# The next layer's first modulation, moved from GpSimd in attention to VectorE in the up projection

## The reference

```
c_act = silu(c)
for l in range(2):
    mod = c_act @ ada_w[l] + ada_b[l]          # ada_w[l] is 1024 x 6144
    sh1, sc1, g1, sh2, sc2, g2 = split(mod, 6)
    h = rmsnorm(x, norm1_g[l]) * (1 + sc1) + sh1
    proj = h @ w_in[l]                          # a scan, a latent attention, a window attention
    y = concat(y_ssd, y_mla, y_swa) @ w_out[l]
    x = x + g1 * y
    h = rmsnorm(x, norm2_g[l]) * (1 + sc2) + sh2
    u = causal_dwconv(h @ ffn_w_up[l])          # width 3, 2 x 2816 channels
    a, b = split(u, 2)
    x = x + g2 * ((silu(a) * b) @ ffn_w_down[l])
return rmsnorm(x, final_norm_g)
```

## Time and profile before

| | |
|---|---|
| three runs, median (lowest to highest) | 2300.6 us (2298.91 to 2301.53) |
| profiled execution | 2302.88 us |
| its span from the first to the last instruction | 2301.1 us |
| mean granted TensorE clock, share of full | 0.988 |
| busy: TensorE, VectorE, ScalarE, GpSimd | 98%, 70%, 48%, 45% |
| DMA traffic | 317.13 MB, mean 138 GB/s |

### The profile page before, as it was taken

One profiled execution on the slowest core, in us unless ns is written; L12 is line 12 of the kernel. 1 busy time (PEld: TensorE's weight loads), 2 busy tenths in 40 slices (PEclk: granted clock), 3 DMA queues, 4 the chain that ended last, 5 costly groups with the idle time before them and its releaser, 6 DMA issues.

```text
span 2301.1 us, 31154 instructions
## 1 busy us (share of the span) xinstructions
PE 2255.3 (98%) x11401; PEld 1852.8 (81%) x11401; DVE 1608.6 (70%) x2242; ACT 1103.9 (48%) x1817; POOL 1027.3 (45%) x664
## 2 busy tenths in 40 slices
PE   6999999999999999999999999999989999999998
PEld 5888878887788888888878787788878888888887
DVE  7885467449866676778898744762796666667886
ACT  5355557434444444444543564772444444444455
POOL 3222369445987777300002224153399777760000
PEclk7999999999999999999999999999999999999999
DMA  9742243342343333477457221224322333337763
GB/s 334 279 135 69 65 119 120 110 141 62 104 128 99 108 104 103 161 278 257 149 193 260 71 69 60 52 83 134 106 78 93 117 94 115 94 129 269 255 203 115
DMA packets 271302, 317.13 MB, mean 138 GB/s; under 512 B 33614, under 2 KB 188033, under 8 KB 270384
## 3 DMA queue, kind: packets, MB, share of 16 engines
q1 hardware_dynamic: 269359, 312.11, 41.8%
q10 hardware_dynamic: 1072, 2.23, 0.4%
q0 software_dynamic: 720, 0.81, 0.1%
HBM read 248.37 MB, written 62.54 MB: 135 GB/s over the span
## 4 chain that ended last, share of the span: by engine, by line
PE 88%; DVE 6%; issue 2%; DMA 1%; SPq 1%; POOL 1%; ACT 0%; DVEq 0%; POOLq 0%; ACTq 0%
PE bank L1579 31%; PE bank L1135 19%; PE bank L1594 17%; PE bank L1192 7%; PE bank L1470 2%; PE bank L1435 1%; PE bank L1351 1%; DVE hLo L2246 1%; PE bank L1398 1%; SPq L539 1%; PE bank L1399 1%; DVE xT L2240 1%; PE bank L1400 1%; PE bank L1391 1%; PE bank L1282 1%
## 5 line engine op out<-in xcount | busy, mean ns | idle before, releaser
L1055 POOL TENSOR_TENSOR wLo<-raw,wHi 128x1024 fp32r<-128x1024 f32 x66 | 164.1, 2487 | 407.3 <-ACT wHi L1057 407.3
L1780 POOL TENSOR_TENSOR prodLo<-comb,prodHi 128x512 fp32r<-128x512 f32 x160 | 234.3, 1471 | 123.8 <-ACT prodHi L1097 123.8
L1579 PE MATMUL bank<-tHi,prodHi 128*128 128x512 f32 x640 | 250.2, 391 | 4.8 <-DVE tLo L2659 4.1
L1579 PE MATMUL bank<-tLo,prodHi 128*128 128x512 f32 x640 | 249.6, 390 | 0.0
L1579 PE MATMUL bank<-tHi,prodLo 128*128 128x512 f32 x640 | 249.5, 390 | 0.0
L1594 PE MATMUL bank<-gateHi,downHi 128*128 128x512 f32 x616 | 240.3, 390 | 0.0
L1594 PE MATMUL bank<-gateHi,downLo 128*128 128x512 f32 x616 | 239.7, 389 | 0.0
L1594 PE MATMUL bank<-gateLo,downHi 128*128 128x512 f32 x616 | 239.7, 389 | 0.0
L1097 ACT ACTIVATE prodHi<-comb 128x512 fp32r<-128x512 f32 x160 | 100.5, 632 | 248.8 <-PE bank L1579 229.5
L2604 DVE SCALAR_TENSOR_TENSOR ub<-bank,ffp,ub 128x1023 f32<-128x1023 f32 x88 | 112.8, 1282 | 141.9 <-ACT ub L2053 140.3
L1579 PE MATMUL bank<-hHi,prodHi 128*128 128x512 f32 x480 | 187.1, 390 | 6.1 <-POOL prodLo L1780 3.5
(11 more groups left out here) (431 smaller groups left out, 5417.1 us busy)
## 6 DMA issues: line engine op xcount, KB each, us to landing
raw<-in_ffn_w_up_dram SPq DMA_DIRECT2D x88, 512.0 KB, 4.8
gateRaw<-gateOut SPq DMA_DIRECT2D x154, 256.0 KB, 4.3
adaE<-in_ada_w_dram SPq DMA_DIRECT2D x64, 512.0 KB, 6.1
gateOut<-gateSums SPq DMA_DIRECT2D x22, 1024.0 KB, 5.5
raw<-in_w_in_dram SPq DMA_DIRECT2D x34, 512.0 KB, 4.2
downRaw<-in_ffn_w_down_dram SPq DMA_DIRECT2D x66, 256.0 KB, 3.7
raw<-in_w_out_dram SPq DMA_DIRECT2D x28, 512.0 KB, 3.8
downCols<-in_ffn_w_down_dram SPq DMA_DIRECT2D x24, 512.0 KB, 3.6
```

The source lines that it names most:

```text
L1055: eng.tensor_tensor(lo[:], raw[slot][:], fview(hi[:]), ALU.subtract).then_inc(s["split_lo"], 1)
L1579: last = mm(o, w[idx][:, c0], moving(idx, kp, hi), start=kp == 0 and q_ == 0, stop=kp == 3 and q_ == 2)
L1780: pool.tensor_tensor(sLoW[idx][:], product_source(js, idx), fview(sHiW[idx][:]), ALU.subtract).then_inc(s["us_lo"], 1)
```

## The change

`load_ada`, `ada_products`, `ada_sum` and their place in attention are taken out. In layer 0's up projection, `load_next` loads 32 blocks of 128 x 512 in pairs behind the other transfers of SyncE's step, `next_product` makes two of them a step on VectorE (js 2 to 17) between result 6 and the taps, and after every eighth turns the sum in 32 x 32 blocks and reduces it to 16 columns. At the end of the stage four matmuls (`next_sums`) sum over the partitions and ScalarE copies 16 columns to `mod`. The new tiles lie in the upper halves of `hLo`, which are free by then, and beside the parameter rows. The stores of rstd for the scan, which stood among the loads of `load_ada`, now stand behind the second output pack in both layers.

```
-NEXT_AT = (23, 24) and load_ada, ada_sum, ada_products with their calls
+NEXT_TILES = 4 * KT
+NEXT_JS = 2
+    nextw = [place(f"nextAda{i}", [P, HALF], F32, R[8 + i] + 2 * K) for i in range(2)]
+    foldN = place("foldNext", [P, 2, 32], F32, at["x"] + 29 * K)
+    nexta = place("nextSum", [P, HALF], F32, R[10] + 2 * K)
+    nextt = place("nextTurned", [P, HALF], F32, R[11] + 2 * K)

+            def load_next(r):
+                c, k = divmod(r, KT)
+                if r < 2:
+                    sp.wait_ge(s["pack_used"], nth("pack_used", D0))
+                else:
+                    sp.wait_ge(s["ada_used"], nth("ada_used", r - 1))
+                sp.dma_start(nextw[r % 2][:], ada_next[:, k * P:(k + 1) * P, c * HALF:(c + 1) * HALF].rearrange("o p m -> (o p) m")).then_inc(s[f"ada_loaded{r % 2}"], 16)

                 load_up(j + 1)
                 if j % 2:
                     store_sums((j - 3) // 2)
+                if onward and 0 <= j - NEXT_JS - 2 < NEXT_TILES // 2:
+                    load_next(2 * (j - NEXT_JS - 2))
+                    load_next(2 * (j - NEXT_JS - 2) + 1)

+            def next_sums():
+                pe.wait_ge(s["ada_part"], nth("ada_part", 9))
+                for r in range(4):
+                    mm(bank[1][32 * r:32 * r + 32, 448:448 + 2 * KT], quad[:], foldN[:].rearrange("p j c -> p (j c)")[:, r:2 * 32:4], start=True, stop=True)

                         pe.wait_ge(s["up_tap"], nth("up_tap", 4 * (FT - 1)))
+                        next_sums()
                         transpose_params(pe, prow1)

                         act.wait_ge(s["params_transposed"], nth("params_transposed", 1))
+                        A(mod[:, 0:2 * KT], bank[1][:, 448:448 + 2 * KT], ACT.Copy).then_inc(s["mod_rest"], 1)

+            def next_product(r):
+                c, k = divmod(r, KT)
+                dve.wait_ge(s[f"ada_loaded{r % 2}"], nth(f"ada_loaded{r % 2}", 16 * (r // 2 + 1)))
+                if k == 0:
+                    dve.tensor_scalar(nexta[:], nextw[r % 2][:], cact[:, 0:1], None, ALU.mult).then_inc(s["ada_used"], 1)
+                else:
+                    dve.wait_ge(s["ada_used"], nth("ada_used", r))
+                    dve.scalar_tensor_tensor(out=nexta[:], in0=nextw[r % 2][:], scalar=cact[:, k:k + 1], in1=nexta[:],
+                                             op0=ALU.mult, op1=ALU.add).then_inc(s["ada_used"], 1)
+                if k == KT - 1:
+                    dve.wait_ge(s["ada_used"], nth("ada_used", r + 1))
+                    link(dve.transpose(nextt[:], nexta[:]))
+                    dve.tensor_reduce(foldN[:, c // 2, 16 * (c % 2):16 * (c % 2) + 16], nextt[:].rearrange("p (c i) -> p c i", i=32),
+                                      AX.X, ALU.add).then_inc(s["ada_part"], 1)

                 if js:
                     result(js - 1, 6)
+                if onward and 0 <= js - NEXT_JS < NEXT_TILES // 2:
+                    next_product(2 * (js - NEXT_JS))
+                    next_product(2 * (js - NEXT_JS) + 1)
                 taps(j - 1, 1)
                 taps(j - 1, 0)
                 result(js, 0)
...
                 if n == 10 and onward:
+                    dve.wait_ge(s["mod_rest"], nth("mod_rest", 2))
                     first_modulation(dve)
```

More of the change, by code:

```diff
@@ L787, in load_pack @@
                     sp.dma_start(raw[n % 2][:].rearrange("p (k m) -> p k m", k=KT), w[:, :, m * P:(m + 1) * P]).then_inc(sem, 16)
[L789 to L802, removed]
             def load_rope_tables():
@@ L896, in _ @@
                     load_rope_tables()
-                    if onward:
-                        load_ada(range(2))
                     place_query_rope()
-                if n == N_OUT0 and onward:
-                    load_ada(range(2, ADA_PACKS))
-                    sp.wait_ge(s["ada_used"], nth("ada_used", ADA_PACKS))
-                if n == N_OUT0 + 2 and not onward:
+                if n == N_OUT0 + 2:
                     store_rstd()
@@ L1193, in half_step @@
                 return last
-            def ada_sum(j, ms=range(KT)):
-                pe.wait_ge(s["ada_used"], nth("ada_used", KT * (j - 3)))
-                acc = (nt[0], nt[1])[j - 4]
-                to = half(2, 1)[:, 384:384 + KT]
-                for m in ms:
-                    last = mm(to[:, m:m + 1], acc[:, m * P:(m + 1) * P], caus01[:, P - 1:P], start=True, stop=True)
-                if ms[-1] == KT - 1:
-                    last.then_inc(s["ada_part"], 1)
+            def next_sums():
+                pe.wait_ge(s["ada_part"], nth("ada_part", 9))
+                for r in range(4):
+                    mm(bank[1][32 * r:32 * r + 32, 448:448 + 2 * KT], quad[:], foldN[:].rearrange("p j c -> p (j c)")[:, r:2 * 32:4], start=True, stop=True)
             def mod_sums(_):
@@ L1422, in transposes @@
                     pe.transpose(half(2, 1)[0:2 * NB, 384:512], rst[:], ident[:])
-                if u in NEXT_AT and onward:
-                    ada_sum(4 + NEXT_AT.index(u))
                 for part in range(2):
@@ L1671, in _ @@
         def _(pool):
-            def ada_products():
-                pool.wait_ge(s["mn_sum"], nth("mn_sum", 1))
-                pool.wait_ge(s["ada_part"], nth("ada_part", 5))
-                for r in range(ADA_PACKS):
-                    j, k = divmod(r, KT)
-                    acc, w = nt[j][:], raw[r % 2][:]
-                    pool.wait_ge(s[f"ada_loaded{r % 2}"], nth(f"ada_loaded{r % 2}", 16 * (r // 2 + 1)))
-                    ck = cact[:, k:k + 1].to_broadcast([P, D])
-                    if k == 0:
-                        pool.tensor_tensor(acc, w, ck, ALU.mult).then_inc(s["ada_used"], 1)
-                    else:
-                        pool.tensor_tensor(w, w, ck, ALU.mult).then_inc(s["ada_prod"], 1)
-                        pool.wait_ge(s["ada_prod"], nth("ada_prod", r - j))
-                        pool.wait_ge(s["ada_used"], nth("ada_used", r))
-                        pool.tensor_tensor(acc, acc, w, ALU.add).then_inc(s["ada_used"], 1)
             def scan_gate(ch):
@@ L2528, in beside_probs @@
                     dve.tensor_copy(rstd_row[:], sums[0:2 * NB, 384:512]).then_inc(s["sd_rstd"], 1)
-                if u in NEXT_AT and onward:
-                    n = NEXT_AT.index(u)
-                    dve.tensor_copy(mod[:, n * KT:(n + 1) * KT], sums[:, 384:384 + KT]).then_inc(s["mod_rest"], 1)
             least(0)
```

13 lines of the change are left out of this document (5 added, 8 removed), and 4 rows, old and new, of the table PER_LAYER.

## The result

The changed kernel takes 2330.14 us (median of 4 runs, 2326.83 to 2332.04), the kernel before 2301.07 us (4 runs, 2298.91 to 2304.38): a ratio of 1.0116, 95% interval [1.0104, 1.0127]. It is slower, and by more than the prediction's range allows (2295 to 2321 us). The execution that was traced (span 2325.1 us) is the fastest of the four, 2326.83 us, so the trace places 24 us of the 29 that the medians show. The three longer runs list a lower mean granted clock, 0.985 to 0.989 against 0.990; no trace places their further 3.3 us.

A forecast was written before the change was run, and what follows sets the result against it. TensorE, busy 98% of the span, was taken as the bound. Stalls 16.1, clock 1.6, end 0.3 and attention -6.9 gave net +11.1 us, 2311.7 on the median; forecast 2311 us, range 2295 to 2321.

The forecast's parts named there:

- Fold steps, 4 x 2.0 = 8.0 us: Up projection, js 5, 9, 13, 17: late loads, two products, transpose and reduction make TensorE wait 2.0 us before product 5.
- The slack: Up projection: result 1 can come 0.6 us late before TensorE waits at product 5; the gate saves about 0.3 us.
- Plain odd steps, 3 x 0.9 = 2.7 us: Up projection, js 7, 11, 15, no transpose or reduction: taps 1.5 us late, costing TensorE 0.9 us each.
- js 2, 3.3 us, and js 3, 2.1 us: Up projection's first two product steps: loads queued behind earlier transfers, GpSimd catching up; stalls of 3.3 and 2.1 us.
- The clock, one fall: Up projection: only the js 2 stall drops TensorE's clock, costing 1.6 us; the 2.0 us stalls do not.
- The fourth rival: Up projection: each 2 us stall also drops the clock, five more falls at 1.6 us, about 2320; chance 0.14.
- Nothing for the even steps, 0.3 us for the end: Up projection: even steps' loads land as VectorE's slot opens, costing nothing; the closing sums and copy cost 0.3 us.
- Attention, -6.9 us: Layer 0 attention: removing one-column matmuls (3.8 us) and two clock falls (1.6 us each) gains 6.9 us; GpSimd's work worth nothing.
- The bounds of the sum: Whole kernel: all unknown costs at one end give -0.8 us, at the other +33 us.
- The first rival: Up projection: loads land in time, only the four folds overrun, so 2294 to 2296.5 us, faster; chance 0.16.
- the lock: Up projection: VectorE's two-SBUF-operand products cannot run beside GpSimd instructions; two take up to 2.7 + 1.3 us, not 1.5.

The follow-up runs named there:

- the kernel with neither: Changed kernel without the up projection's loads, products and folds (small fills instead), so attention has neither GpSimd's modulation work nor TensorE's sums: 2295.11 us, ratio 0.9967.

## Why the prediction was wrong in size

The direction, the place and the main mechanism were right: loads behind the store of the sums, VectorE's slot overrun, product 5 late in the steps named. What failed is the size of the stalls, with the count of the clock's falls that hangs on it, and one path that was put at nothing. The sum said +11.1 us on the profiled execution and the profiles show +24.0.

- **Fold steps, 4 x 2.0 = 8.0 us.** Measured 3.0, 3.0, 4.3 and 3.0, together 13.3. This is the term most mis-sized. Its late start of the taps was 2.9 us and measured 4.0 in js 5: the data came 0.7 us later behind the opening of the slot (3.24 us against 2.5), the two products took 3.15 us against 2.8, and the fold its 1.4 us as predicted. The loads landed 5.3 us after issue, where the working had 4.4. (By its own rows, a landing of the store at 674.7 against 674.1, it should have added 0.6 us from last byte to signal and not 0.4.) The slack was predicted well: 4.0 late and 3.0 waited leaves 1.0, predicted 0.9.
- **Plain odd steps, 3 x 0.9 = 2.7 us.** Measured 3 x 1.55 = 4.7: late by 2.55 us in js 7 (the taps at 720.15), against 1.5.
- **js 2, 3.3 us, and js 3, 2.1 us.** Measured 4.1 and 0.5 (a step of 19.52 us, with idle time of 0.2): about 0.8 less than the sum that was said, and otherwise divided.
- **The clock, one fall.** This step failed in kind: "I count a fall for it, 1.6 us as above, and none for the 2.0 us stalls". The stalls were of 3 us, and four waits came with a fall in place of one: 6.1 us against 1.6. The fourth rival ("each stall of 2 us drops the clock as well", about 2320) named it at a chance of 0.14; what rows 14 show of waits of 2.06 and 2.07 us, one of two with a fall, left it open.
- **Nothing for the even steps, 0.3 us for the end.** The end measured 0.4. The even steps from js 4 to 16 are 19.1 to 19.4 us long in place of 19.04, 1.1 us together. Their pairs landed within 0.2 us of the slot's opening or before it, as said (though 684.66 + 1 + 4.9 + 0.4 is 691.0, not the 691.7 given), and TensorE lost all the same. The path is one that the prediction put at nothing: it asked what GpSimd does to VectorE's products, not what they do to GpSimd's chain and through it to the gate. In the run with early loads, where there is nothing else, it costs most of 392.5 - 388.5 = 4.0 us.
- **Attention, -6.9 us.** Measured -8.7 in the stage; 1.6 of the difference is a fall of the clock at 346 us that the profiled execution of before had and the changed one did not. The part behind row group 2, 33.24 us, was right. But "TensorE waited for none of them ... they are worth nothing" fails, though its first half is right in the kernel before: GpSimd's work was worth 2.3 us (from the kernel with neither) to 3.0 us (from the kernel before). And the two falls of the clock, put down to the sums, did not come with the sums alone.

Against the prediction the waits add 6.0 us, the clock 4.5, and what no term held 4.1 (the rest of the 32.6 us, 4.4, less the 0.3 of the end); attention gives back 1.8 more. That is 12.8 of the 12.9 us. The medians differ by 5 us more than the profiles; those runs have no trace.

The bounds of the sum (+33 at the upper end) held this; the range, cut at 2321, did not. The first rival (loads in time, 2294 to 2296.5) was built as an experiment: with the loads early the kernel takes 2300.08, since that rival lacked GpSimd's part.

On the lock the trace and the runs agree with the prediction's row: median 1.59 us for a product of 0.75, also with the data long there (1.59 in the run with early loads). By the Trainium skill (SBUF — State Buffer, "SBUF: two separate sides") the ports shared by the two are an exclusive lock; the traces agree, and show that it delays both: GpSimd's 1.29 us became 1.75 beside the products. What stays open: why the loads of js 13 land 1.1 us later than those of js 5, and why the wait at 769.81 alone did not drop the clock.

## What to carry to other kernels

Work that fits an engine's idle time must also have its data by then: look at what stands ahead of its loads in the queue and at what the queue waits for there, and put the work at the place with the most time behind the landing, not at the one with the widest gap. Here moving 32 products to the end of VectorE's step, some 14 to 17 us later, turned 1.0116 into 0.9972. Where two engines hold each other up, follow both chains: the one that starts late is seen at once, the one that is stretched by 0.7 us shows only half a step later, as 0.3 us in each of 11 steps. And a stall's price is its length plus what the clock does: steps with a wait of 1.55 us grew by 1.8 us, one with 3.0 us and no fall by 3.3, two with 3.0 us and a fall by 4.6 and 4.8.

## What was not expected of the hardware

- Two products of VectorE with SBUF operands cost GpSimd 0.73 us over two instructions of 1.29, and the same two products, one 1.18 and one 0.74 us with a PSUM instruction between, cost it 0.43.
- A pair of 256 KB loads landed as long after its issue behind a 1 MB store (5.3 and 5.4 us in js 5) as right behind 1 MB of weight loads (5.4 and 4.9 us in js 4), and putting it ahead of the store left that as it was (5.6 and 5.0 us). With neither close ahead the median was 2.7 us, in the run with early loads.
- Groups of one-column matmuls (32 records, median 250 ns) ran at full clock in the one trace without GpSimd's work beside them; the falls of the kernel before at 401 and 408 us did not come back in the trace of any kernel that lacked either half.
